# A two-block model on one core: half-row filter products, roots on ScalarE, spread row operations, first head reordered

## The chip, the cores and the metric

The kernel runs on one core of one Trainium2 chip. The metric is device time in microseconds of one execution. The kernel before has a median of 2186.13 us over three runs.

## What is computed

All of it is float32, on 256 rows (latents) and, in the second block, 256 more (context), 1024 columns wide. The first block has two layers of feed-forward, hybrid mixer, feed-forward, each followed by a layer norm; the second has an even layer (a long convolution with a learned filter, and attention) and an odd layer (an mLSTM with eight heads).

```python
for l in range(DEPTH):                                  # first block
    x = layer_norm(ALPHA * x + 0.5 * swiglu(x, w1[l, 0], w2[l, 0]))
    x = layer_norm(ALPHA * x + hybrid_mixer(x, ...))
    x = layer_norm(ALPHA * x + 0.5 * swiglu(x, w1[l, 1], w2[l, 1]))
# second block, layer j:  h = rms_norm(x, g_pre) * (1 + sc) + sh
#   y = even_mixer(h) or odd_mixer(h);  x = x + ga * rms_norm(y, g_post)
def hyena_filter(...):
    hdn = sin(fr * (z @ w1 + b1)); hdn = sin(fr * (hdn @ w2 + b2))
    h = (hdn @ w3).reshape(n, 2, HY_WIDTH)              # w3: 64 x 2048
```

## The kernel before

**Precision.** A large product is made of three matmuls on two parts of each operand: high weights by high features, high by low, low by high. The high part is a rounded copy made on ScalarE (`weights_hi`, line 1497), the low part a subtraction on VectorE (`weights_lo`, line 2071), both for one half block of weights (128 x 2048) at a time. Small products are plain float32, which the trace shows as two passes, each a weight load and a matmul (line 1003).

**Weights and order.** 147 blocks of weights of 2 MB come through a ring of three in the order of use, on SyncE's queue. TensorE's program is one fixed order of half blocks. `after(l, key)` in the programs of ScalarE and VectorE makes the part of the half that takes the slot of the one named; so their place between other work sets when TensorE finds its weights. A half of a block is 48 matmuls of 256 columns or 24 of 512.

**First block.** `ffn` runs eleven pairs of up halves, then eleven down halves (`rows`, line 919). In the mixer VectorE ends the recurrence with `split(hg_hi, hg_lo)`, then runs `rows_gained(l, 0)` (lines 2162 to 2173: the previous norm's gain and bias on two tiles of 1024 columns, four operations in one piece; the end counts `rows_ok`, for which GpSimd waits before it loads the next rows into `bcast`), then the low parts at "yg" 3, 4 and 5. In `ffn` the same piece stands ahead of pair 2. A layer norm takes its root on ScalarE (`row_root`, Sqrt, then a Newton step on VectorE, lines 2116 to 2125).

**Filter network.** `filters(q)` stands between the down halves of the last feed-forward. f1 and f2 are products with 64 output rows, each followed by the sine (range reduction on VectorE, Sin on ScalarE); f3 makes 2 x 4 products of 64 rows into 512 columns (line 1003), for q = 4 and 5.

**Even layer's start.** The roots of the four row tiles come from `root` (lines 2378 to 2389: eleven small VectorE operations, three Newton steps). ScalarE and VectorE scale the rows (`erow`), TensorE transposes them (`turn_all`, line 1097), ScalarE and VectorE make `xt`, ScalarE `x2_hi`, VectorE `x2_lo` (line 2412). `tile_t` (lines 1068 to 1072) then runs high by high and high by low for each k, and the low weights at the end; the first tile waits for `x2_lo` of each k. `x2_hi` lies over the spectra's sources.

**Between the layers.** `post` takes two roots with `root`, the second with the next layer's sums of squares; ScalarE's `squares` and `row_squares` come before. `turn_segment(0)` (line 1111) transposes the rows, `gate_columns` (lines 1349 to 1351) is the first product behind.

**First head.** VectorE computes the gates' logarithm, a low part, waits for `gate_rows` (ScalarE's three copies, in `ml_in(0)`), runs scans (2727 to 2742) with one low part among them, and only then the first head's short convolution (2763 to 2775). ScalarE's Tanh on its result (`ml_silu(0)`) stands at the end of `ml_gates(0)`. Then come the last products for q and k (2779, 2780), `qk_done`, and TensorE's scores (line 1003).

**Start.** Before the first layer VectorE computes softplus of `a_param` as a series of small operations (`log1p`), for which ScalarE runs one Exp.

## Time and profile before

| | before |
|---|---|
| median of three runs | 2186.13 us (2181.99 to 2194.47) |
| profiled execution | 2188.97 us |
| its span | 2187.2 us |
| TensorE matmul, weight load | 2145.6 us (98%), 1945.9 us (89%) |
| VectorE, ScalarE, GpSimd | 1431.6 us (65%), 900.1 us (41%), 18.1 us (1%) |
| moved by DMA | 348.94 MB, mean 160 GB/s |

In the profile PE is TensorE's matmuls, PEld its weight loads, DVE VectorE, ACT ScalarE, POOL GpSimd. Matmuls overlap and their ends are modelled, so a duration in a row is longer than the distance to the next one. A number in square brackets is the idle time ahead of the row and what ended it. PEclk is the share of TensorE's full clock that was granted.

### The profile page before, as it was taken

The numbers are of one execution on the slowest core, as the hardware profiler recorded it, in microseconds if no ns is written. First come the engines' busy times: TensorE is split into PE (matmuls) and PEld (weight loads), VectorE is DVE, ScalarE is ACT, GpSimd is POOL, SyncE is SP. The second block draws the span as 40 slices with busy tenths as digits, with TensorE's granted clock in tenths as the row PEclk, the third lists the DMA queues.
The fourth block names the chain that finished last, engine by engine and source line by source line (L and its number), as shares of the span: only waits on it lengthen the run. The fifth ranks groups of instructions, "written<-read, shape, count | busy, mean of one in ns | idle before, by whom it ended". The sixth has DMA issues, their size and how long they took to land. (4 is left out here: it accounts for less than half of the span.)

```text
span 2187.2 us, 35415 instructions
## 1 busy us (share of the span) xinstructions
PE 2145.6 (98%) x14986; PEld 1945.9 (89%) x14986; DVE 1431.6 (65%) x2084; ACT 900.1 (41%) x1060; POOL 18.1 (1%) x35
## 2 busy tenths in 40 slices
PE   9999999999999999999999999999999989999998
PEld 8998999999989989999899768888788878999996
DVE  5556877685566548876765677877666456666665
ACT  4333365343343334383433353222344334443442
POOL 0000000000000000000000000000000000000000
PEclk9999999999999999999999999999999999999999
DMA  9654555666566555455564432222112232232331
GB/s 346 228 181 186 193 193 200 233 259 232 183 257 235 193 193 191 179 180 203 217 240 185 159 129 77 77 77 77 65 52 78 87 116 78 97 136 78 116 116 58
DMA packets 28925, 348.94 MB, mean 160 GB/s; under 512 B 2976, under 2 KB 5408, under 8 KB 8352
## 3 DMA queue, kind: packets, MB, share of 16 engines
q1 hardware_dynamic: 24672, 313.42, 38.8%
q0 software_dynamic: 4096, 33.26, 3.8%
q8 instruction: 119, 1.95, 0.4%
q14 instruction: 38, 0.31, 0.0%
HBM read 345.62 MB, written 1.05 MB: 158 GB/s over the span
## 5 line engine op out<-in xcount | busy, mean ns | idle before, releaser
L2071 DVE TENSOR_TENSOR w_lo<-ring,w_hi 128x2048 fp32r<-128x2048 f32 x290 | 661.8, 2290 | 417.6 <-ACT w_hi L1497 413.0
L1497 ACT ACTIVATE w_hi<-ring 128x2048 fp32r<-128x2048 f32 x290 | 555.7, 1917 | 700.0 <-PE banks L778 472.3
L773 PE MATMUL banks<-x_hi,w_hi 128*128 128x256 f32 x2112 | 505.2, 280 | 0.2 <-ACT w_hi L1497 0.2
L774 PE MATMUL banks<-x_lo,w_hi 128*128 128x256 f32 x2112 | 504.2, 280 | 0.0
L773 PEld LDWEIGHTS banks<-x_hi,w_hi 128*128 128x128 f32 x2112 | 399.2, 189 | 1.1 <-issue 1.1
L774 PEld LDWEIGHTS banks<-x_lo,w_hi 128*128 128x128 f32 x2112 | 399.5, 189 | 0.0
L778 PE MATMUL banks<-x_hi,w_lo 128*128 128x256 f32 x2112 | 288.8, 279 | 7.9 <-DVE w_lo L2071 7.9
L778 PEld LDWEIGHTS banks<-x_hi,w_lo 128*128 128x128 f32 x2112 | 264.5, 189 | 8.7 <-DVE w_lo L2071 8.7
L1068 PE MATMUL banks<-x_hi,w_hi 128*128 128x512 f32 (+1 forms) x664 | 236.8, 370 | 1.2 <-DVE x_lo L2412 1.2
L1069 PE MATMUL banks<-x_lo,w_hi 128*128 128x512 f32 (+1 forms) x664 | 229.1, 358 | 0.0
L1531 ACT ACTIVATE arena<-banks 128x512 f32<-128x512 f32 (+5 forms) x178 | 79.7, 471 | 284.4 <-PE banks L1072 165.2
L1068 PEld LDWEIGHTS banks<-x_hi,w_hi 128*128 128x128 f32 x664 | 125.1, 188 | 23.2 <-DVE x_lo L2412 3.5
L1072 PE MATMUL banks<-x_hi,w_lo 128*128 128x512 f32 (+1 forms) x664 | 143.6, 358 | 0.8 <-DVE w_lo L2071 0.8
L1069 PEld LDWEIGHTS banks<-x_lo,w_hi 128*128 128x128 f32 x664 | 125.0, 188 | 19.4 <-issue 0.2
L919 PE MATMUL banks<-w_hi,gt_hi 128*128 128x512 f32 x352 | 138.8, 394 | 0.0
L919 PE MATMUL banks<-w_hi,gt_lo 128*128 128x512 f32 x352 | 138.4, 393 | 0.0
L1003 PE MATMUL banks<-arena 128*128 128x256 f32 (+3 forms) x576 | 127.2, 372 | 4.1 <-DVEq L2781 4.1
L1072 PEld LDWEIGHTS banks<-x_hi,w_lo 128*128 128x128 f32 x664 | 111.2, 188 | 21.8 <-DVE w_lo L2071 1.0
L1003 PEld LDWEIGHTS banks<-arena 128*128 128x128 f32 x576 | 99.4, 191 | 25.4 <-issue 9.5
L1082 PE MATMUL banks<-w_hi,x_hi 128*128 128x256 f32 x416 | 103.1, 286 | 0.0
L1083 PE MATMUL banks<-w_hi,x_lo 128*128 128x256 f32 x416 | 100.3, 279 | 0.0
L919 PE MATMUL banks<-w_lo,gt_hi 128*128 128x512 f32 x352 | 89.4, 393 | 0.0
(367 smaller groups left out, 2808.4 us busy)
## 6 DMA issues: line engine op xcount, KB each, us to landing
ring<-weights SPq DMA_DIRECT2D x147, 2048.0 KB, 7.8
arena<-mods POOLq DMA_DIRECT2D x11, 2048.0 KB, 11.6
bcast<-lnrows POOLq DMA_DIRECT2D x12, 512.0 KB, 10.0
ring<-weights SPq DMA_DIRECT2D x2, 1024.0 KB, 9.9
xrow<-x SPq DMA_DIRECT2D x1, 1024.0 KB, 5.2
arena<-hy_consts POOLq DMA_DIRECT2D x1, 1024.0 KB, 15.4
xrow<-ctx_rows POOLq DMA_DIRECT2D x1, 1024.0 KB, 5.3
out<-xrow SPq DMA_DIRECT2D x4, 256.0 KB, 2.0
```

The lines of the kernel that those rows point to most:

```text
L773: nc.tensor.matmul(out, hi[:, k, t * P:(t + 1) * P], x_h[:, k, :], start=k == 0, stop=False)
L774: nc.tensor.matmul(out, hi[:, k, t * P:(t + 1) * P], x_l[:, k, :], start=False, stop=False)
L778: mm = nc.tensor.matmul(out, lo[:, k, t * P:(t + 1) * P], x_h[:, k, :], start=False, stop=k == KT - 1)
L919: mm = nc.tensor.matmul(out, g[:, k, r * P:(r + 1) * P], w[:, u, :], start=k == 0 and p == 0 and not low, stop=k == depth - 1 and low)
L1003: mm = nc.tensor.matmul(out, lhs, rhs, start=n == 0, stop=n == len(pairs) - 1)
L1068: nc.tensor.matmul(out, hi[:, k, part_], x2_hi[:, k, cols_], start=k == 0, stop=False)
L1069: nc.tensor.matmul(out, hi[:, k, part_], x2_lo[:, k, cols_], start=False, stop=False)
L1072: mm = nc.tensor.matmul(out, lo[:, k, part_], x2_hi[:, k, cols_], start=False, stop=k == KT - 1)
L1082: nc.tensor.matmul(out, x2_hi[:, k, rows_], hi[:, k, :], start=k == 0, stop=False)
L1083: nc.tensor.matmul(out, x2_lo[:, k, rows_], hi[:, k, :], start=False, stop=False)
L1497: nc.scalar.activation(hi, raw, ACT.Copy).then_inc(w_hi_done, 1)
L2071: v.tensor_tensor(lo, raw, hi.bitcast(F32), ALU.subtract).then_inc(w_lo_done, 1)
```

## The change

- **Filter network.** The filter weights are loaded twice, into rows 0 to 63 and 64 to 127, by a second DMA on GpSimd's queue; TensorE waits for both. f1 and f2 are computed twice, into either half of the rows of the bank; the sine works on all 128 rows. The f3 products alternate: c = 0 and 2 on the first 64 rows of the array, 1 and 3 on the others.
- **First products.** The first tile of the even layer runs all high by high as `x2_hi` comes, then the low weights, then high by low; `gate_columns` runs both products with `x2_hi` for each k, then high by low.
- **Roots.** `root_of` replaces `root` at three places: ScalarE takes Sqrt (`dev_copy`), VectorE the reciprocal and one Newton step. A Sqrt on one column is put ahead of `squares("even_y", 1)`, an Exp on one column ahead of the gates' exponential.
- **Row operations.** `rows_gained` becomes `row_gained`, one operation behind each of four low parts: pairs 2 and 3 in `ffn`, "yg" 3 and 4 in the mixer.
- **Series.** The softplus series moves from the start to the down halves 0 to 3 of the first feed-forward (`decay_series`), its Exp with it.
- **First head.** `qk_conv(0)` stands ahead of the wait for `gate_rows`, `ml_silu(0)` behind ScalarE's copies in `ml_in(0)`; the head's gate columns stay where they were.

```diff
@@ -733,7 +734,8 @@
-                        pool.dma_start(filt_sb[0:HY_HIDDEN, :], filt).then_inc(S2["hy_in"], 16)
+                        for rows_ in twice:
+                            pool.dma_start(filt_sb[rows_, :], filt).then_inc(S2["hy_in"], 16)
@@ -960,19 +962,22 @@
-                    pe.wait_ge(S2["hy_in"], 48)
+                    pe.wait_ge(S2["hy_in"], 64)
-                    group(banks[0:HY_HIDDEN, b, 0:SEQ], [(hy_w1, hy_zt)], done=b)
+                    group(banks[twice[0], b, 0:SEQ], [(hy_w1, hy_zt)])
+                    group(banks[twice[1], b, 0:SEQ], [(hy_w1, hy_zt)], done=b)
-                    group(banks[0:HY_HIDDEN, b, 0:SEQ], [(hy_w2, sin_out[0])], done=b)
+                    group(banks[twice[0], b, 0:SEQ], [(hy_w2, sin_out[0][twice[0], :])])
+                    group(banks[twice[1], b, 0:SEQ], [(hy_w2, sin_out[0][twice[0], :])], done=b)
-                        group(banks[:, b, :], [(sin_out[1][:, t * P:(t + 1) * P], hy_w3[:, c * 512:(c + 1) * 512])],
+                        group(banks[:, b, :], [(sin_out[1][twice[c % 2], t * P:(t + 1) * P],
+                                                hy_w3[c % 2][:, c * 512:(c + 1) * 512])],
@@ -1062,9 +1067,18 @@
+                if ready is not None:
+                    for k in range(KT):
+                        pe.wait_ge(S2["x2_hi"], k + 1)
+                        nc.tensor.matmul(out, hi[:, k, part_], x2_hi[:, k, cols_], start=k == 0, stop=False)
+                    lo_ready(h)
+                    for k in range(KT):
+                        nc.tensor.matmul(out, lo[:, k, part_], x2_hi[:, k, cols_], start=False, stop=False)
+                    for k in range(KT):
+                        ready(k)
+                        mm = nc.tensor.matmul(out, hi[:, k, part_], x2_lo[:, k, cols_], start=False, stop=k == KT - 1)
+                    return mm
-                    if ready is not None:
-                        ready(k)
@@ -1345,10 +1359,13 @@
+                        pe.wait_ge(S2["x2_hi"], KT + 4 * w + k // 2 + 1)
+                    nc.tensor.matmul(out, gw_hi[:, k, :], x2_hi[:, k, cols_], start=k == 0, stop=False)
+                    nc.tensor.matmul(out, gw_lo[:, k, :], x2_hi[:, k, cols_], start=False, stop=False)
+                for k in range(KT):
+                    if k % 2 == 0:
-                    nc.tensor.matmul(out, gw_hi[:, k, :], x2_hi[:, k, cols_], start=k == 0, stop=False)
-                    nc.tensor.matmul(out, gw_hi[:, k, :], x2_lo[:, k, cols_], start=False, stop=False)
-                    mm = nc.tensor.matmul(out, gw_lo[:, k, :], x2_hi[:, k, cols_], start=False, stop=k == KT - 1)
+                    mm = nc.tensor.matmul(out, gw_hi[:, k, :], x2_lo[:, k, cols_], start=False, stop=k == KT - 1)
@@ -1524,6 +1541,9 @@
+                    if (l, f, q) == (0, 0, 0):
+                        act.wait_ge(sp_abs, 1)
+                        nc.scalar.activation(small[:, 16:32], small[:, 0:16], ACT.Exp).then_inc(sp_exp, 1)
@@ -1660,6 +1678,11 @@
+            def dev_copy(dst, var, n):
+
+                act.wait_ge(S2["root_in"], n)
+                copy(dst, var, S2["root_out"], ACT.Sqrt)
+
@@ -1683,6 +1706,7 @@
+            dev_copy(rs[:, 12:16], rs[:, 24:28], 1)
@@ -1821,6 +1845,8 @@
+                    if (seg, h, r) == ("even_y", 1, 1):
+                        dev_copy(rs[:, 12:14], rs[:, 24:26], 2)
@@ -1830,6 +1856,7 @@
+            copy(floor[:, 0:1], ones[:, 0:1], None, ACT.Sqrt)
@@ -1840,6 +1867,7 @@
+            dev_copy(rs[:, 12:16], rs[:, 24:28], 3)
@@ -1870,6 +1898,7 @@
+            copy(floor[:, 0:1], ones[:, 0:1], None, ACT.Exp)
@@ -1886,6 +1915,7 @@
+                    ml_silu(0)
@@ -1905,7 +1935,6 @@
-                    ml_silu(0)
@@ -2159,24 +2188,23 @@
-            def rows_gained(l, n):
-
-                filled(dve, l, "layer", "turn", n, 3)
-                dve.wait_ge(row_in, 32 * (3 * l + n) + 32)
-                for r in range(RT):
-                    v.tensor_tensor(xrow[:, r, :], xrow[:, r, :], bcast[:, 0, :], ALU.mult)
-                v.drain()
-                for r in range(RT):
-                    x = v.tensor_tensor(xrow[:, r, :], xrow[:, r, :], bcast[:, 1, :], ALU.add)
-                x.then_inc(S2["rows_ok"], 1)
-                v.drain()
+            def row_gained(l, n, r, step):
+
+                if r + step == 0:
+                    filled(dve, l, "layer", "turn", n, 3)
+                    dve.wait_ge(row_in, 32 * (3 * l + n) + 32)
+                v.drain()
+                x = v.tensor_tensor(xrow[:, r, :], xrow[:, r, :], bcast[:, step, :], (ALU.mult, ALU.add)[step])
+                if r + step == 2:
+                    x.then_inc(S2["rows_ok"], 1)
+                    v.drain()
-                    if j == 2 and l + f:
-                        rows_gained(*((l, 1) if f else (l - 1, 2)))
-                    after(l, "up", f, j, 0)
-                    after(l, "up", f, j, 1)
+                    for side in range(2):
+                        after(l, "up", f, j, side)
+                        if j in (2, 3) and l + f:
+                            row_gained(*((l, 1) if f else (l - 1, 2)), side, j - 2)
@@ -2205,25 +2235,44 @@
...
+            def decay_series(step):
+                if step == 0:
+                    v.scalar_tensor_tensor(both(0), ap, -1.0, ap, ALU.mult, ALU.min).then_inc(sp_abs, 1)
+                if step == 1:
+                    dve.wait_ge(sp_exp, 1)
+                if step == 3:
...
@@ -2333,10 +2365,11 @@
-                rows_gained(l, 0)
+                        if q < 5:
+                            row_gained(l, 0, side, q - 3)
@@ -2375,6 +2408,20 @@
+            def root_of(y, v_, d, u, n):
+
+                v.tensor_scalar(u, v_, -0.5, None, ALU.mult)
+                v.drain().then_inc(S2["root_in"], 1)
+                dve.wait_ge(S2["root_out"], n)
+                v.reciprocal(y, d)
+                v.drain()
+                v.tensor_tensor(d, y, y, ALU.mult)
+                v.drain()
+                v.tensor_tensor(d, d, u, ALU.mult)
+                v.drain()
+                v.scalar_tensor_tensor(y, d, 1.5, y, ALU.add, ALU.mult)
+                v.drain()
+
@@ -2395,7 +2442,7 @@
-            root(rs[:, 28:32], rs[:, 24:28], rs[:, 12:16], rs[:, 8:12])
+            root_of(rs[:, 28:32], rs[:, 24:28], rs[:, 12:16], rs[:, 8:12], 1)
@@ -2637,13 +2684,13 @@
-                        root(rs[:, 4:8], rs[:, 24:28], rs[:, 12:16], rs[:, 8:12])
+                        root_of(rs[:, 4:8], rs[:, 24:28], rs[:, 12:16], rs[:, 8:12], 3)
-                        root(y, mean, rs[:, 12:14], rs[:, 14:16])
+                        root_of(y, mean, rs[:, 12:14], rs[:, 14:16], 2)
@@ -2723,6 +2770,25 @@
+            def qk_conv(i):
+                v.tensor_copy(ml_c[:, 0:MLC], c2[:, i * MLC + C2["ml"]:(i + 1) * MLC + C2["ml"]])
+                if i:
+                    head_gates(i)
+                v.drain()
+                released(dve, i, "ml", "q")
...
+                v.drain().then_inc(S2["qk_conv"], 1)
+                dve.sem_inc(S2["copied"], 1)
+            qk_conv(0)
@@ -2760,21 +2826,8 @@
-                v.tensor_copy(ml_c[:, 0:MLC], c2[:, i * MLC + C2["ml"]:(i + 1) * MLC + C2["ml"]])
-                    head_gates(i)
-                v.drain()
...
-                dve.sem_inc(S2["copied"], 1)
+                    qk_conv(i)
```

## Rows read from the trace of the kernel before

**Rows 1.** The page: busy time of each engine, share of the span, instructions.
```profile
PE 2145.6 (98%) x14986; PEld 1945.9 (89%) x14986; DVE 1431.6 (65%) x2084; ACT 900.1 (41%) x1060; POOL 18.1 (1%) x35
```
**Rows 2.** Waits of PE: who waited for whom, us in total, times, longest.
```profile
PE banks L778 <- DVE w_lo L2071: 7.9, 4, 3.6
PE banks L1111 <- ACT arena L1531: 5.4, 1, 5.4
```
**Rows 3.** First head, in order of time: start, us, engine, line, tiles.
```profile
1823.45 1.21 DVE L2727 TENSOR_TENSOR_SCAN arena<-arena 32x512 f32<-32x512 f32 x1 [2.38 <-ACTq L1887]
...
1828.09 2.29 DVE L2071 TENSOR_TENSOR w_lo<-ring,w_hi 128x2048 fp32r<-128x2048 f32 x1
...
1830.44 0.39 PE L1072 MATMUL banks<-x_hi,w_lo 128*128 128x256 f32 x1 [0.83 <-DVE w_lo L2071]
...
1833.95 0.17 DVE L2763 COPY arena<-c 128x10 f32<-128x10 f32 x1 [0.16 <-issue]
...
1839.83 0.48 PE L1003 MATMUL banks<-arena 128*128 128x256 f32 x1 [4.05 <-DVEq L2781]
```
**Rows 4.** Stretches: us, busy (records) of PE, PEld, DVE, ACT, POOL, then PEclk.
```profile
362.20:365.60 3.40, 3.40 (x18) 3.40 (x17) 3.34 (x2) 0.00 (x0) 0.00 (x0) 0.50 0.48 184
365.60:369.00 3.40, 3.40 (x32) 3.40 (x31) 0.24 (x1) 2.19 (x3) 0.00 (x0) 1.00 0.49 96
...
1785.60:1795.80 10.20, 7.43 (x32) 6.85 (x33) 7.57 (x13) 7.41 (x13) 0.00 (x0) 0.50 0.52 223
...
1840.20:1843.60 3.40, 3.40 (x11) 2.74 (x10) 3.32 (x9) 0.00 (x0) 0.00 (x0) 0.50 0.26 111
```
**Rows 5.** Layer 0's mixer, in order of time.
```profile
353.96 2.36 DVE L2167 TENSOR_TENSOR xrow<-xrow,bcast 128x1024 f32<-128x1024 f32 x2
...
358.85 2.29 DVE L2071 TENSOR_TENSOR w_lo<-ring,w_hi 128x2048 fp32r<-128x2048 f32 x1
...
361.19 0.39 PE L778 MATMUL banks<-x_hi,w_lo 128*128 128x256 f32 x1 [3.57 <-DVE w_lo L2071]
```
**Rows 6.** Layer 1's mixer, in order of time.
```profile
991.90 0.39 PE L778 MATMUL banks<-x_hi,w_lo 128*128 128x256 f32 x1 [3.29 <-DVE w_lo L2071]
```
**Rows 7.** Between the layers, in order of time.
```profile
1782.99 0.17 DVE L2380 TENSOR_SCALAR rs<-rs 128x4 f32<-128x4 f32 x1
...
1785.50 1.15 ACT L1531 ACTIVATE arena<-xrow,rs 128x1024 f32<-128x1024 f32 x1 [2.49 <-DVEq L2641]
...
1786.70 3.68 PE L1111 MATMUL banks<-cr,arena 128*128 128x128 f32 x16 [5.43 <-ACT arena L1531]
```
**Rows 8.** A layer norm's root, VectorE in order of time.
```profile
441.00 0.14 DVE L2117 TENSOR_SCALAR rstd<-mv 128x1 f32<-128x1 f32 x1
441.44 0.16 DVE L2121 RECIPROCAL rstd<-rstd 128x1 f32<-128x1 f32 x1 [0.30 <-ACT rstd L1531]
```
**Rows 9.** Even layer's start, ScalarE in order of time.
```profile
1283.53 1.15 ACT L1531 ACTIVATE arena<-xrow,rs 128x1024 f32<-128x1024 f32 x1 [1.61 <-DVEq L2399]
...
1296.58 1.15 ACT L1531 ACTIVATE x_hi<-xt 128x512 fp32r<-128x512 f32 x2
```
**Rows 10.** ScalarE in order of time: a table load, and idle at two places.
```profile
1264.19 1.28 ACT L1531 ACT_TABLE_LOAD   x1
...
1771.20 0.60 ACT L1531 ACTIVATE z<-banks 128x512 f32<-128x512 f32 x1 [0.77 <-PE banks L1262]
...
1813.98 0.26 ACT L1531 ACTIVATE arena<-arena 128x64 f32<-128x64 f32 x1 [3.23 <-DVEq L2704]
```
**Rows 11.** PE in order of time: a filter burst, and the last modulation rows.
```profile
1230.96 3.70 PE L1003 MATMUL banks<-filt_sb,arena 64*128 64x512 f32 x8
...
1779.34 1.93 PE L876 MATMUL banks<-ring,cond 128*2 128x128 f32 x64
```
**Rows 12.** Two stretches of PE alone: us, busy (records), PEclk, DMA share, GB/s.
```profile
250.00:270.00 20.00, 20.00 (x179) 1.00 0.57 211
1170.00:1190.00 20.00, 20.00 (x172) 1.00 0.51 199
```

More of the change, by code:

```diff
@@ L410, in build @@
         top[0] = FT * SEQ * 2
-        sin_out, sin_in = ([part(SEQ)[0:HY_HIDDEN, :] for _ in range(2)] for _ in range(2))
+        sin_out, sin_in = ([part(SEQ) for _ in range(2)] for _ in range(2))
         mod_at = (SBUF_END - arena_at) // 32 * 8 - 512
@@ L447, in build @@
         hy_w2 = filt_sb[0:HY_HIDDEN, SEQ + HY_HIDDEN:SEQ + 2 * HY_HIDDEN]
-        hy_w3 = filt_sb[0:HY_HIDDEN, SEQ + 2 * HY_HIDDEN:FILTCOLS - 4]
+        twice = [slice(HY_HIDDEN * j, HY_HIDDEN * (j + 1)) for j in range(2)]
+        hy_w3 = [filt_sb[rows_, SEQ + 2 * HY_HIDDEN:FILTCOLS - 4] for rows_ in twice]
         hyf = filt_sb[:, FILTCOLS - 4:FILTCOLS]
@@ L1561, in _ @@
             copy(cond[:].rearrange("p a b -> p (a b)"), c2[:, C2["cond"]:C2["cond"] + 16], S2["cond_done"], ACT.Silu)
-            act.wait_ge(sp_abs, 1)
-            nc.scalar.activation(small[:, 16:32], small[:, 0:16], ACT.Exp).then_inc(sp_exp, 1)
             for l in range(DEPTH):
@@ L2195, in ffn @@
                     after(l, "down", f, q // 2, q % 2)
+                    if l + f == 0 and q < 4:
+                        decay_series(q)
                     if q == FT // 4:
@@ L2206, in split, with both @@
                 return v.tensor_tensor(dst_lo, src, dst_hi.bitcast(F32), ALU.subtract)
-            def log1p(dst, y, tmp, tmp2):
-                v.tensor_scalar(tmp, y, 2.0, None, ALU.add)
-                v.drain()
-                v.reciprocal(tmp, tmp)
-                v.drain()
-                v.tensor_tensor(tmp, tmp, y, ALU.mult)
-                v.drain()
-                v.tensor_tensor(tmp2, tmp, tmp, ALU.mult)
-                v.drain()
-                v.tensor_scalar(dst, tmp2, 2.0 / 17.0, 2.0 / 15.0, ALU.mult, ALU.add)
-                for odd in (13.0, 11.0, 9.0, 7.0, 5.0, 3.0, 1.0):
+            lcs = colsb[:].rearrange("p (l c) -> p l c", l=DEPTH)
+            ap = lcs[:, :, LCOL["a_param"]:LCOL["a_param"] + 8]
+            def both(n):
+                return small[:, 16 * n:16 * n + 16].rearrange("p (l k) -> p l k", l=DEPTH)
+            def decay_series(step):
+                dst, y, tmp, tmp2 = (small[:, 16 * n:16 * n + 16] for n in (3, 1, 4, 5))
+                if step == 0:
+                    v.scalar_tensor_tensor(both(0), ap, -1.0, ap, ALU.mult, ALU.min).then_inc(sp_abs, 1)
+                    v.tensor_scalar(half_bs[:], lcs[:, :, LCOL["rg_b"]:LCOL["rg_b"] + 16], 0.5, None, ALU.mult)
+                    v.tensor_scalar(half_ms[:], lcs[:, :, LCOL["b_merge"]:LCOL["b_merge"] + 16], 0.5, None, ALU.mult)
+                    v.tensor_scalar(both(2), ap, -1.0, 0.0, ALU.mult, ALU.max)
+                if step == 1:
+                    dve.wait_ge(sp_exp, 1)
+                    v.tensor_scalar(tmp, y, 2.0, None, ALU.add)
+                    v.drain()
+                    v.reciprocal(tmp, tmp)
+                    v.drain()
+                    v.tensor_tensor(tmp, tmp, y, ALU.mult)
+                    v.drain()
+                    v.tensor_tensor(tmp2, tmp, tmp, ALU.mult)
+                    v.drain()
+                    v.tensor_scalar(dst, tmp2, 2.0 / 17.0, 2.0 / 15.0, ALU.mult, ALU.add)
+                for odd in ((), (), (13.0, 11.0, 9.0, 7.0), (5.0, 3.0, 1.0))[step]:
                     v.drain()
```

48 lines of the change are left out of this document (19 added, 29 removed).

## The prediction

> **What bounds the kernel now.** I read the page first. TensorE is busy 98% of the 2187.2 us span; no other engine passes 65% [rows 1]. So only two things can shorten this kernel: TensorE's own work, and the moments in which it stands still or runs slowly. The chain of waits on the page says the same: it stays on TensorE. Next I listed TensorE's waits by releaser. The reader should see how few and how long they are: four waits of matmuls for the low part of the weights, 7.9 us together, one wait of 5.4 us before the transposes of L1111 [rows 2], one of 4.1 us before the first head's scores [rows 3]. Last I asked for the granted clock around each. After the wait at 361 us, and again after the 5.4 and the 4.1 us waits, it is 0.50, that is 1.2 instead of 2.4 GHz, for 3.4, 10.2 and 3.4 us [rows 4]. A stall is thus paid once in waiting and, mostly, a second time in slow matmuls. Eighteen matmul records stand in the 3.4 us after the first, 32 in the next 3.4: nearly half of such a stretch, 1.7 us, is lost each time that TensorE has dense work to do.
>
> The sum below is made against the profiled execution's own time, 2188.97 us (span 2187.2). The median of the three runs is 2186.13, 2.8 less.
>
> **Row operations, layers' mixers.** Before, `rows_gained(l, 0)` puts four operations on 1024 columns on VectorE in one piece, 353.96 to 358.85, and only then the weights' low part, whose first operation (2.29 us) ends at 361.1; the matmul waits 3.57 us for it and starts at 361.19 [rows 5]. The change puts one row operation (about 1.2 us) behind each of four low parts. The low part then starts at 354.0 and ends at 356.3. TensorE came to it at 361.19 - 3.57 = 357.6, so nothing is left of the wait; the cover left is 1.3 us. The next low part starts 1.2 us after that and ends near 359.8, three microseconds before its use, since one half of a block lasts 5.4 us on TensorE. What is late next there is nothing before the next layer norm. Layer 0 gives 3.6 us and the 1.7 us of clock; layer 1 has the same wait, 3.29 us, without a fall of the clock [rows 6]. In the feed-forward loops the same split hides a block that nobody waited for: none of the long waits is there, so 0. GpSimd's next load of the norm rows waits for `rows_ok`, now some 10 us later; it had to wait only for the next layer norm, over 50 us away, so 0. Sum: **8.6 us**.
>
> **Roots on ScalarE.** The old `root` runs from its first operation at 1782.99 to ScalarE's use at 1785.50: 2.51 us [rows 7]. For the new one the layer norms have the pattern already: from the last scalar operation (441.00) over ScalarE's Sqrt to the reciprocal (441.44) takes 0.44 us [rows 8]. Reciprocal, two products and one more are four steps of 0.25, and the signal to ScalarE 0.28, as in the old one: about 1.5 us. Each root is 1.0 us shorter.
> - First root, before `turn_all`: ScalarE's row copy moves from 1283.53 to about 1282.5 [rows 9]. ScalarE now waits for the deviation ahead of its copies of the second spectrum, so their bank comes free 0.5 us later, about when TensorE wants it. The transposes start 1.0 us earlier.
> - But then the products' new order decides. ScalarE's last high part (the pair begins at 1296.58) ended at 1297.7, and after it the old order had one pair and eight low-weight products left, through 1301.0. The new order has seventeen left, 17 x 0.233 = 4.0 us. With everything 1.0 us earlier this ends at 1300.8: gain **0.2 us**, bounds -0.8 and 1.0.
> - Second and third root, between the layers: the second is off the path, since ScalarE's sums of squares hold up the third. The third starts the transposes 1.0 us earlier (from 1786.70 [rows 7]). The gate columns get the same new order: twelve products instead of six stand behind the last high part. At half clock (0.215 us each) that eats the gain, at full clock about 1.6 us stay. I take **0.5 us**, near the lower end since the stall of over 4 us that remains is still longer than the one at 361 us which lowered the clock; bounds -0.5 and 1.8.
> - New table loads: Sqrt ahead of the second half's squares, Exp ahead of the gates' exponential. A load is 1.28 us; the first meets 0.77 us of idle ahead of the square of 1771.20 and delays that one alone, whose reader is busy with a low part until 1772.7; the second meets 3.23 us of idle [rows 10]. 0.
>
> **First head.** VectorE waited 2.38 us for ScalarE's copies before its scan at 1823.45, and did the head's convolution only at 1833.95, 3.7 us of it (until ScalarE's Tanh at 1837.8); the scores started at 1839.83 after 4.05 us of waiting [rows 3]. The change runs the convolution (3.7 us) in that gap. The scan moves to about 1824.85, 1.4 us later, and with it all behind it on VectorE: the low part of 1828.09, for which TensorE already waited until 1830.44. So the new wait there is about 2.4 us in place of 1.0. Then the head's gates end at 35.3, the two last products of queries and keys at 36.5, while TensorE, 1.4 us later too, wants the scores at 37.05: no wait. Scores start 2.8 us earlier. ScalarE's high parts behind the moved Tanh come 2.3 us later, one of them 0.2 us after TensorE could use it; covered by the same wait. The fall of the clock at 1840.2 [rows 4] goes with its wait, 1.6 us. Sum **4.4 us**; lower bound 2.5, if the wait of 2.4 us pulls the clock down in its turn.
>
> **Filter network.** Eight products of 64 rows run as sixteen passes in two bursts. One burst, from 1230.96, takes 3.70 us by its row, 3.6 without the modelled end of its last pass: eight passes of 0.45 us [rows 11]. The change puts alternate products on the other 64 rows. What two parts of the array do at the same time is seen at L876: 64 passes on four column parts take 1.93 us, where one after the other, at 128 columns each, they would take four times that [rows 11]. If rows behave like columns, 3.6 us become 1.9 (four places of 0.45 and the start of the second part) and both bursts give 3.4 us. Against it stand the two first products, now computed twice: nothing if they overlap, 0.6 us each if not. I take **3.2 us**; bounds -1.2 and 3.4.
>
> The Trainium skill speaks against this term: "TensorE: Matmul & The Clock Gate", Part 3, says that matmuls start and end in strict order. By it the second pass of a product holds back the next product, five slots are needed where four would do, and the term is about 2.4 us. The trace's L876 has two passes to each product and shows no such hold, so I keep the row's value. The page "TensorEngine Tiling (Array Packing)", Key Properties, adds that a change of mode drains the engine; no run here shows that price apart, and the old code changes mode here as often.
>
> **Elsewhere.** The decay series leaves the start for the first down products. No wait of TensorE follows the series at the start, the four of [rows 2] are at 324, 361, 955 and 991 us; and in the down products VectorE has over 3 us free in each 5.5 us half. 0, bounds 0 and 0.3. The second copy of the filter weights is one more load on GpSimd's queue, 90 us ahead of its use. 0.
>
> Sum: 8.6 + 0.2 + 0.5 + 4.4 + 3.2 = 16.9 us. From the profiled time 2172.1; from the median 2169.2. One of the two clock losses that go, in layer 0 but not in layer 1, may be missing in the median run, so I put the forecast between them: **2170.5 us**.
>
> **The rivals.**
> - *The halves of the rows run one after the other, and the head's new wait lowers the clock.* Minus 3.2 and 0.6 more for the doubled products, minus 1.7: 11.4 us gained, 2176.2. For it: no row shows row parts. Chance 0.18.
> - *Matmuls in strict order.* The filter term falls by 0.8 us: 2171.3. By the skill's rule above; against it L876. 0.10.
> - *The pace of the products goes down (slower than before).* The same products run at two paces at full clock: 20 us hold 179 matmul records near 250 us and 172 near 1170 us [rows 12], 4% apart. The pace changes where something short stands between products, so a change of order can move it. Fast stretches of 256 columns are about 410 us of the trace (both mixers mostly); all at the lower pace, with the 512-column ones (365 us, 2%), costs 23 us: 2193. It decides from 17 us on, that is from about three quarters of these stretches. 0.05.
> - *The pace goes up.* About 500 us of feed-forward and mixer go at the lower pace; all at the higher is 19 us less: 2152. 0.05.
> - *The low part is still late in the mixers*, because TensorE runs into a later one: the 8.6 us stay, 2179. Against it the 1.3 us of cover above. 0.06.
>
> **How the numbers follow.** Forecast 0.56, with a range of its own of 2165 to 2176. The rivals at 2176 and 2179 are taken in, the two of the pace for the most part not: **2160 to 2181**. About 0.5%, 11 us, is what a measurement of this kernel tells from no change, so faster means under 2175.2. Faster: forecast and strict order 0.60, a third of the first rival 0.06, pace up 0.05, in all 0.71. Same 0.25. Slower by over 0.5%: 0.04.
>
> **What would show it.** In the changed profile: no matmul of L778 waiting over 1 us near 357 and 984; the granted clock 1.0 there; the passes of a filter burst within 2 us; the first head's long wait replaced by one of 2 to 3 us for the low part, ten microseconds earlier; the wait before the transposes near 4.4 us with the clock still falling; 172 or 179 records in 20 us in the same stretches as before. A lower pace in a mixer, or a new wait for ring loads, would make the prediction wrong.

## The result and the profile after

The changed kernel takes 2170.86 us in the median of 8 runs (2165.54 to 2175.98), the kernel before 2186.22 beside it. The ratio is 0.992, with a 95% interval from 0.9901 to 0.9938: 15.4 us less, where 2170.5 was forecast. The profiled execution took 2168.66 us, its span is 2166.9, so the first pair of profiles lies 20.3 us apart, 5 more than the medians. Where these 5 come from is the first question of the experiments.

TensorE's waits in the changed kernel, by releaser: us in total, times, longest. The two long waits for the low part of [rows 2] are gone, and so is the wait before the first head's scores.

```profile
PE banks L1125 <- ACT arena L1551: 4.3, 1, 4.3
PE banks L792 <- ACT w_hi L1514: 2.3, 1, 2.3
PE banks L1086 <- DVE w_lo L2100: 2.1, 1, 2.1
PE banks L1073 <- ACT x_hi L1551: 2.0, 2, 1.1
...
PE banks L1363 <- ACT x_hi L1551: 1.8, 2, 1.2
...
PE banks L780 <- DVE w_lo L2100: 1.0, 2, 0.5
```

L1125 is the old L1111, 5.4 before; the 2.1 us are the first head's new wait. The two rows of 2.0 and 1.8 us are new: they wait for ScalarE's high parts, in the two places where the order of the products was changed.

VectorE in layer 0's mixer. The row operations of [rows 5] now stand one behind each low part, and each low part ends before its use.

```profile
353.10 2.29 DVE L2100 TENSOR_TENSOR w_lo<-ring,w_hi 128x2048 fp32r<-128x2048 f32 x1
355.48 1.22 DVE L2197 TENSOR_TENSOR xrow<-xrow,bcast 128x1024 f32<-128x1024 f32 x1
356.62 2.28 DVE L2100 TENSOR_TENSOR w_lo<-ring,w_hi 128x2048 fp32r<-128x2048 f32 x1
359.00 1.23 DVE L2197 TENSOR_TENSOR xrow<-xrow,bcast 128x1024 f32<-128x1024 f32 x1
```

Stretches of the changed kernel: us, busy (records) of PE, PEld, DVE, ACT, POOL, then PEclk, DMA share, GB/s. Where TensorE stood still before, in layer 0's mixer, the clock is 1.00. But in the even layer's first tile there is a fall that the kernel before did not have, and between the layers the clock is down for 13.7 us and not 10.2 [rows 4].

```profile
354.00:358.00 4.00, 4.00 (x37) 4.00 (x37) 3.91 (x3) 2.65 (x3) 0.00 (x0) 1.00 0.63 266
...
1279.60:1283.00 3.40, 3.40 (x10) 2.63 (x9) 2.40 (x4) 2.09 (x3) 0.00 (x0) 0.51 0.02 5
1767.70:1781.40 13.70, 10.52 (x47) 9.90 (x48) 10.05 (x30) 9.48 (x14) 0.00 (x0) 0.50 0.50 213
```

A filter burst in the changed kernel, and the doubled first product. Eight passes take 1.92 us to the next matmul, where [rows 11] had 3.6; four passes of f1 have 0.65 us, against 0.64 for the two before.

```profile
1193.18 0.65 PE L1008 MATMUL banks<-filt_sb 33*64 33x256 f32 x4
```
```profile
1216.73 1.99 PE L1008 MATMUL banks<-filt_sb,arena 64*128 64x512 f32 x8
1218.65 0.50 PE L921 MATMUL banks<-w_hi,gt_hi 128*128 128x512 f32 x1
```

**Where the time went.** I set each matmul of one trace beside the same matmul of the other and took the difference of their starts. From it I took out the pace of the products: what a product of 256 columns takes over 113.3 ns, or one of 512 over 229, when it lies within 110 to 122 or 225 to 240 ns. That pace alone is 32.2 us in the first profile of the kernel before and 27.5 in the changed one's. The rest, in us ahead of the first profile of before (the three columns ahead of the last are experiments below; the line "all" also holds 0.4 us less between 950 and 985 us in all four, which is the first profile's own):

```
stretch                        forecast  b_again  b_rows  b_filt_head  changed
start, to 345 us                  0.0      0.5     -0.1       0.1        0.6
layer 0's mixer                   5.3     -0.9      5.5       0.0        5.5
layer 1's mixer                   3.3     -2.9      3.6      -1.6        3.6
filter network                    3.2      0.0      0.0       3.4        3.4
even start: to the transposes     1.0      0.0      0.0       0.0        1.2
even start: first tile           -0.8      0.0      0.0       0.0       -2.4
between layers: to transposes     1.0      0.0      0.0       0.0        1.2
between layers: gate columns     -0.5      0.4      0.1      -0.2       -1.5
first head, from 1803 us          4.4     -0.8      0.0       4.3        4.4
all, with what lies between      16.9     -4.5      8.6       6.0       15.6
pace of the products              0.0      4.3      4.7       6.3        4.7
```

So the 20.3 us of the first pair are 15.6 us of changes and 4.7 of pace.

Two things on how to read the runs below. They were taken in five sets on several chips, each with runs of the kernel before beside it; the ratio is always to those. And the medians of the same changed kernel in two sets differ by 5.7 us, so a term of one to three microseconds is read from the traces, not from a median.

### The profile page after: what moved, and what is told of

Same layout as the page of the kernel before. It is cut to its first block, busy times and chain, and to the rows that moved or that the text cites. A ratio compares the mean times of both kernels' runs of the same rounds, so it can differ in the third digit from the quotient of the medians.

```text
span 2166.9 us, 35416 instructions
## 1 busy us (share of the span) xinstructions
PE 2136.0 (99%) x14990; PEld 1938.4 (89%) x14990; DVE 1429.6 (66%) x2066; ACT 902.2 (42%) x1066; POOL 18.8 (1%) x36
## 4 chain that ended last, share of the span: by engine, by line
PE 94%; DVE 2%; ACT 2%; DVEq 1%; issue 0%; ACTq 0%
PE banks L921 13%; PE banks L780 12%; PE banks L775 12%; PE banks L776 12%; PE banks L1008 8%; PE banks L1086 6%; PE banks L1083 6%; PE banks L1082 6%; PE banks L792 2%; PE banks L1100 2%; PE banks L1096 2%; PE banks L1097 2%; PE banks L1277 2%; PE banks L1276 2%; PE banks L1278 2%; PE banks L878 1%
```

## The experiments

**The kernel before, once more.** No edit.

> The kernel before, unchanged, profiled once more. In the first pair of profiles the changed kernel is 20.3 us ahead, in the medians 15.4. 4.5 us of the 20.3 come in the feed-forward loops, where no order changed and only the distance of the products differs (114.8 against 117.8 ns). Theory A, the pace is a draw of each execution: this profile shows other stretches at the lower pace than the first one, its span differs from 2187.2 by up to 5 us, and aligned with the first profile the difference lies in the feed-forward loops. Theory B, the pace belongs to the program: the same stretches, and the span within 1 us of 2187.2. In both, the fall of the clock after the 3.5 us wait of the first layer's mixer: there again by theory of a rule (a wait of that length always lowers it), gone by the theory that it depends on the phase.

Measured: 2188.43 us (12 runs, 2184.51 to 2191.91), ratio 1.0011 (0.9999 to 1.0022). The same stretch of the same program, first in the first profile, then in this one (columns as above):

```profile
660.00:680.00 20.00, 20.00 (x172) 20.00 (x172) 16.12 (x12) 6.78 (x6) 1.05 (x2) 1.00 0.50 176
```
```profile
660.00:680.00 20.00, 20.00 (x179) 20.00 (x178) 15.24 (x14) 8.48 (x6) 1.05 (x2) 1.00 0.48 172
```

The reader should see 172 and 179 matmul records at the same granted clock: the pace of a stretch can differ between two executions of one program, as theory A says. It happens that the spans agree to 0.1 us, since 4.3 us of better pace stand against 4.5 of other losses. Of these, 3.8 us went in the mixers to falls of the clock: after the wait in layer 0's mixer it was down for 6.8 us instead of 3.4, and after the one in layer 1's for 6.8 where the first profile had none. And there was a wait that the first profile lacks, of 1.8 us at the start:

```profile
33.81 0.85 PE L778 MATMUL banks<-x_hi,w_lo 128*128 128x256 f32 x5 [1.80 <-DVE w_lo L2071]
```

VectorE was at the decay series until 31.4 us. In this execution the clock rose earlier in the first microseconds (0.8 us gained) and did not fall at 14 us (1.6 us): TensorE was 2.4 us further by 18 us, and so it ran into the series.

**The changed kernel, once more.** No edit.

> The changed kernel, unchanged, profiled once more. Theory A (pace is a draw): span 2162 to 2173, other stretches at the lower pace than in its first profile. Theory B (pace belongs to the program): span within 1 us of 2166.9, same stretches. The fall of the clock in the first tile of the even layer (1279.6, 3.4 us at 0.50) and the 13.7 us at 0.50 between the layers: both again if the new orders of products cause them, one of them missing if they hang on the phase.

Measured: 2165.12 us (4 runs, 2163.95 to 2166.81), ratio 0.9911 (0.9894 to 0.9928). The span is 2165.0. The pace differs in the first 200 us; from there on nearly the same stretches are at the lower pace as in the first profile, and the sums are 27.4 and 27.5 us. That half of theory A's forecast failed: the pace can differ between executions, but here it mostly repeated. The 1.9 us between the spans are the start. Both falls are there again, 3.4 us in the first tile and 13.7 between the layers. The clock stayed up at the start, TensorE was 2.0 us ahead at 20 us, and kept it: there is no wait at 33 us here. All 12 runs of the changed kernel together have a median of 2167.7 us; its distance from before is 15.4 us in one set and 20.6 in the other.

**The row operations alone.** Before, with:

```diff
-                rows_gained(l, 0)
                 for q in (3, 4, 5):
                     for side in range(2):
                         after(l, "yg", q, side)
+                        if q < 5:
+                            row_gained(l, 0, side, q - 3)
```
(and the same in the feed-forward).

> The kernel before with the row operations spread, and nothing else. My theory: the waits of 3.6 and 3.3 us for the low part in the two mixers are gone, nothing is late in their place; aligned with a profile of the kernel before, 3.6 us (5.3 where that profile has a fall of the clock there) are gained in layer 0's mixer, 3.3 in layer 1's, 0 in the feed-forward loops beside the pace of the products. In time 7 to 9 us less than before. Rival: the spread is what moved the pace in the feed-forward loops of the changed kernel (4.5 us): then the loops are faster here too, in all 11 to 14 us less.

Measured: 2175.38 us against 2185.74, ratio 0.9956 (0.9941 to 0.9971), 10.4 us less. By the trace 5.5 and 3.6 us, and 0 in the feed-forward loops once the pace is taken out. The rival falls: the pace here (27.5 us) is also that of the untouched kernel's second profile (27.9). That the median gained more than 8.6 would fit the falls after layer 1's wait (of the three traces with the old mixer, the next experiment's being the third, two have one there), but six runs do not show it.

**Filter network and first head alone.** Before, with the diff's edits of `filters`, of the filter weights' DMAs and of the sine, and with these lines, whose old places are emptied:

```diff
+            qk_conv(0)
             dve.wait_ge(S2["gate_rows"], 1)
...
                     A.drain().then_inc(S2["gate_rows"], 1)
                     act.sem_inc(free[b], 1)
+                    ml_silu(0)
```

> The kernel before with the filter network's halves and the first head's new order, and nothing else; the two lie 600 us apart and are read apart in the trace. My theory: the filter bursts take 1.9 us each instead of 3.6 and the doubled first products cost nothing, 3.4 to 3.5 us gained; the first head gains 3.9 to 4.5 us (scores without a wait, the low part's wait 2.1 instead of 0.8), and no fall of the clock. In time 7 to 8 us less than before. Rival for the head: without the roots' change in front the head starts in another phase, the 2.1 us wait lowers the clock, and only 2.5 us remain.

Measured: 2178.31 us against 2185.74, ratio 0.9972 (0.9957 to 0.9987), 7.4 us less. By the trace the filters give 3.4 us and the head 4.3; the wait of 2.1 us did not lower the clock. Both as expected. The two filter bursts:

```profile
1226.24 1.99 PE L1008 MATMUL banks<-filt_sb,arena 64*128 64x512 f32 x8
...
1233.87 1.99 PE L1008 MATMUL banks<-filt_sb,arena 64*128 64x512 f32 x8
```

**The old orders of products.** The changed kernel, with:

```diff
-                if ready is not None:
-                    for k in range(KT):
-                        pe.wait_ge(S2["x2_hi"], k + 1)
...
                 for k in range(KT):
+                    if ready is not None:
+                        ready(k)
                     nc.tensor.matmul(out, hi[:, k, part_], x2_hi[:, k, cols_], start=k == 0, stop=False)
                     nc.tensor.matmul(out, hi[:, k, part_], x2_lo[:, k, cols_], start=False, stop=False)
```
(and `gate_columns` as before).

> The changed kernel with the old order of products in both places: the first tile of the even layer takes high by high and high by low together and the low weights last, and so do the gate columns. The roots on ScalarE stay. Theory A, the new orders cost the two losses (first tile -2.4 us behind transposes that start 1.15 earlier, gate columns -1.5 behind transposes 1.15 earlier): aligned with the changed kernel, 2.0 to 2.4 us are gained in the first tile, half of it since the clock does not fall there, and 0.5 to 1.2 between the layers, where the stretch at 0.50 is back to 10.2 us. Theory B, the clock falls there by the phase alone: it falls here too and at most 0.6 us are gained in the first tile.

Measured: 2166.77 us (6 runs, 2157.45 to 2172.48), ratio 0.9916 (0.9894 to 0.9938). Against the changed kernel's trace 2.4 us are gained in the first tile and 1.6 between the layers, where the clock is down for 10.2 us again: theory A. The median shows none of it: it lies between those of the changed kernel's two sets (2165.12 and 2170.86). In the trace, 1.6 us went at another place, where the clock fell after the first head's 2.1 us wait; how often it does so in the unprofiled runs is not known.

```profile
1804.70:1808.10 3.40, 3.40 (x19) 3.40 (x18) 2.96 (x6) 0.42 (x1) 0.00 (x0) 0.53 0.00 0
```

**The three kinds of product interleaved.** The changed kernel, with:

```diff
-                    for k in range(KT):
-                        pe.wait_ge(S2["x2_hi"], k + 1)
...
+                    for k in range(0, KT, 2):
+                        for a in (k, k + 1):
+                            pe.wait_ge(S2["x2_hi"], a + 1)
+                            nc.tensor.matmul(out, hi[:, a, part_], x2_hi[:, a, cols_], start=a == 0, stop=False)
...
+                        for a in (k, k + 1):
+                            nc.tensor.matmul(out, lo[:, a, part_], x2_hi[:, a, cols_], start=False, stop=False)
+                        for a in (k, k + 1):
+                            ready(a)
+                            mm = nc.tensor.matmul(out, hi[:, a, part_], x2_lo[:, a, cols_], start=False, stop=a == KT - 1)
```
in the first tile; `gate_columns` takes each pair's high by low once the next pair's products with the high part are issued.

> The changed kernel with the three kinds of product interleaved by pairs of k in both places, so that after ScalarE's last high part only six products are left in the first tile (16 in the changed kernel) and eight in the gate columns (12). If TensorE has work at hand between the high parts, its waits of 0.9 and 1.1 us in the first tile mostly fill and the clock stays at 1.00: the first tile ends 3.5 to 4.5 us earlier than in the changed kernel, the gate columns 0.8 to 1.5 us. If the clock falls all the same: 2.5 and 0.8. Time 3 to 5 us below the changed kernel.

Measured: 2166.13 us (6 runs, 2161.3 to 2179.52), ratio 0.992 (0.9893 to 0.9947). First tile 4.4 us earlier, no fall there. Gate columns 0.1, not 0.8 to 1.5: the clock is down for 13.7 us, as in the changed kernel. Half the expectation failed, and the median is not 3 to 5 us below the 2167.7 of the changed kernel's 12 runs. The clock fell after the head's wait here too.

**Order of the last filter products, and the series back at the start.** The changed kernel, with:

```diff
-                        group(banks[:, b, :], [(sin_out[1][twice[c % 2], t * P:(t + 1) * P],
-                                                hy_w3[c % 2][:, c * 512:(c + 1) * 512])],
+                        part = 0 if t else c // 2
+                        group(banks[:, b, :], [(sin_out[1][twice[part], t * P:(t + 1) * P],
+                                                hy_w3[part][:, c * 512:(c + 1) * 512])],
```
and `decay_series(0..3)` before the first layer.

> The changed kernel with two edits 1200 us apart. First, the order of the last filter products: in the first burst the two products of the first half of the rows stand next to each other, then the two of the second half; in the second burst all four are on the first half. Halves that work at the same time only when neighbours in the program differ (strict order): first burst 3.0 to 3.6 us, with one overlap in the middle; halves that run ahead of each other freely: 1.9 us as in the changed kernel. Second burst 3.6 us in either case, 1.7 more. Second edit, the decay series is back before the first layer: no wait of TensorE changes there, 0; the 0.6 us which the changed kernel was ahead at 20 us stay or go with the clock's phase and not with the series.

Measured: 2172.56 us against 2184.67, ratio 0.9944 (0.9924 to 0.9964). The two bursts:

```profile
1220.19 1.99 PE L1009 MATMUL banks<-filt_sb,arena 64*128 64x512 f32 x8
1222.11 0.51 PE L921 MATMUL banks<-w_hi,gt_hi 128*128 128x512 f32 x1
...
1227.83 3.70 PE L1009 MATMUL banks<-filt_sb,arena 64*128 64x512 f32 x8
1231.46 0.50 PE L921 MATMUL banks<-w_hi,gt_hi 128*128 128x512 f32 x1
```

With the products of one half next to each other in the program the burst takes the same 1.92 us: the halves run ahead of each other. All on one half takes 3.63. The second edit went against the expectation of 0. As in the untouched kernel's second profile the clock stayed up at the start, TensorE reached the low part early, and waited for the series; then the clock fell: TensorE was 2.4 us ahead of the first profile of before at 30 us and 2.2 behind at 40, so 4.6 us were lost.

```profile
34.19 1.08 PE L780 MATMUL banks<-x_hi,w_lo 128*128 128x256 f32 x7 [2.79 <-DVE w_lo L2100]
```

**The roots back on VectorE.** The changed kernel, with `root` for `root_of` at the three places, and without `dev_copy` and the two operations on one column.

> The changed kernel with all three roots back on VectorE and without the two table loads ahead; the new orders of products stay. Each root is 1.0 us longer, the transposes start 1.15 us later in both places. First tile: its end is set by ScalarE's last high part and the 16 products behind it, so 1.0 to 1.2 us are lost, and the fall of the clock stays if the order of the products is its cause. Between the layers 1.0 to 1.2 us are lost in the wait before the transposes (5.4 instead of 4.3), and no gain stands against it. Rival: ScalarE's wait for the deviation was itself a cost, and less than 0.6 is lost at the first place.

Measured: 2171.76 us against 2184.67, ratio 0.9938 (0.9918 to 0.9958). The transposes start 1.0 us later at the first place and 1.15 at the second: the rival falls. But the first tile then ends 0.6 us ahead of the changed kernel's, since with the same new order the clock did not fall:

```profile
1278.60:1283.00 4.40, 3.51 (x11) 1.70 (x9) 3.99 (x8) 3.82 (x8) 0.00 (x0) 1.00 0.00 0
```

Between the layers the low clock came in two pieces, 3.4 and 6.8 us, and the gate columns lost 2.0 us behind the transposes, where the changed kernel lost 1.5.

So the fall in the first tile costs 1.6 us and the order by itself 0.8. The order makes it likely, not certain: four traces have the new order there and three of them the fall; of five with the old order and five interleaved none has it.

**Toward a better kernel.** The changed kernel with the interleaved first tile (first edit of a_inter) and the old gate columns (second edit of a_order).

> The changed kernel with the first tile's products interleaved by pairs of k and the gate columns in their old order. What two runs gained apart should add: 4.4 us in the first tile (no fall of the clock there) and 1.6 between the layers (10.2 us at 0.50 instead of 13.7), 6 us against the changed kernel beside the pace of the products and the falls of the clock elsewhere. In time 2160 to 2165 us. If the gate columns' gain hung on the phase of the clock and not on the order, only 4.4.

Measured: 2166.26 us (5 runs, 2164.46 to 2168.55), ratio 0.9915 (0.9902 to 0.9928). Against the changed kernel's trace 4.4 us are gained in the first tile and 1.0 between the layers, not 1.6 (10.2 us at the low clock); the pace was 2.4 us worse and the start 0.5.

**The wait between the layers filled.** The same, with (the products write a bank that the transposes then overwrite):

```diff
             mod_row(8, 0)
-            turn_segment(0)
+            take(pe, 0, "odd", "pre", 0, 0)
+            for _ in range(36):
+                nc.tensor.matmul(banks[:, plan["odd"]["pre", 0, 0][0], 0:P], ident, ident, start=True, stop=True)
+            turn_segment(0, True)
```
(`True`: the bank is already taken).

> As the kernel with both of these orders, and 36 products of 128 columns whose result nobody reads fill TensorE's wait of 4.3 us between the layers. If the wait is what lowers the clock, it stays at 1.00 through the transposes and the gate columns: the transposes take 1.9 us instead of 3.7, the twenty-four products of each half run at 0.12 instead of 0.215 us, and behind ScalarE's and VectorE's steps 2.5 to 4 us are left at the first products of the next layer. If the clock falls all the same, the fillers change nothing, or cost up to 1 us where they outlast the wait.

Measured: 2170.96 us, ratio 0.9933 (0.9918 to 0.9948). The clock stays at 1.00, but each filler is two passes: they last 8.2 us and delay the transposes by 3.8. From there to the first products of the next layer 3.0 us are gained on the changed kernel, against 1.0 without fillers; in all it is 1.8 us behind the kernel without fillers, and the median too is higher.

**The same fillers, the gate columns interleaved.**

> The kernel with both places interleaved, and the same 36 products in the wait between the layers. At the full clock the order of the gate columns costs nothing any more: the old order waits 1.7 us for the low part first, the interleaved one starts with ScalarE's high part and has eight products left behind the last. If the clock stays at 1.00 it is 0 to 1 us ahead of the filled kernel with the old order; if the new order lowers the clock by itself (its waits lie between products), it falls during the gate columns and 1 to 2 us are lost.

Measured: 2164.95 us, ratio 0.9915 (0.9897 to 0.9933). From the transposes 2.2 us are gained, 0.8 less than with the old order: the clock falls for 3.4 us at 1770, in the gate columns. That is the second outcome, but one trace does not show that the order does it: with the old order TensorE waits longer there, in two pieces of 2.2 and 1.4 us, and the clock stayed up. The waits in the gate columns, first here, then in the next experiment's trace:

```profile
PE banks L1368 <- ACT x_hi L1556: 3.1, 2, 1.9
```
```profile
PE banks L1368 <- DVE x_lo L2722: 3.6, 2, 2.5
```

The median goes the other way than the 0.8 us, 6 us below that of the fillers with the old order. In the two traces the pace makes 6.1 us in that direction; that the same holds in the other runs is not shown.

**Half as many fillers, old gate columns.**

```diff
-            for _ in range(36):
+            for _ in range(18):
```

> The filled kernel with 18 instead of 36 products. The 36 ran as 72 passes of 0.113 us, 8.2 us, and delayed the transposes by 3.8; eighteen take 4.1 us and end inside the wait of 4.3. If the clock stays at 1.00 as it did with 36: transposes on time, then 1.7 us gained in them, and 1.0 to 1.5 in the gate columns, in all 2.7 to 3.2 us against the changed kernel between 1762 and 1787 us, where the kernel with the same orders and no fillers gained 1.0. If a shorter filling lets the clock fall all the same: 1.0 as without fillers. The first tile gains its 4.4 us again. In time 2160 to 2165 us, since the pace of the products moves single executions by more than these terms.

Measured: 2160.5 us (4 runs, 2153.66 to 2161.56) against 2187.05, ratio 0.9876 (0.9858 to 0.9895). That is 26.5 us below the kernel before. The changed kernel was not run beside it; its ratios were 0.992 and 0.9911, so this one is probably faster, by four runs. The fillers and the transposes, TensorE in order of time, and the stretch behind:

```profile
1751.11 4.29 PE L1356 MATMUL banks<-cr 128*128 128x128 f32 x36
1755.47 1.97 PE L1127 MATMUL banks<-cr,arena 128*128 128x128 f32 x16
```
```profile
1756.50:1770.00 13.50, 9.93 (x83) 9.54 (x82) 10.69 (x31) 9.49 (x14) 0.00 (x0) 1.00 0.33 139
```

The transposes start on time and take 1.97 us instead of 3.68 [rows 7]; 2.9 us are gained there and 4.4 in the first tile. Without fillers the same orders gained 1.0, so filling the wait is worth 1.9 us. This trace, of the fastest of the four runs, is 15.0 us ahead of the changed kernel's first: beside these, 7.0 us are pace and 2.1 a start without a fall, and 1.6 are lost by a fall after the first head's wait.

## Why the forecast came out

The median was met to 0.4 us, the sum only in part, and that closeness is luck in three ways. The forecast took about 1.3 us off the sum because layer 0's fall of the clock might be missing in the median run; the runs gave no reason for that (in b_again the clock was down after both mixers' waits, for 6.8 us each, and b_rows gained 10.4 us in the median). The two reordered places gave 2.2 us less than forecast, and nobody expected the small gains elsewhere. And the sample: the changed kernel's second set has 2165.12. Point by point:

- **Row operations.** Right in mechanism and size: 5.5 and 3.6 us for 5.3 and 3.3, b_rows alone, nothing late behind. What the argument from one profile missed is that the fall after such a wait is not a property of the place: layer 1's wait of 3.3 us had none in the first profile, 3.4 us in b_filt_head's and 6.8 in b_again's. The median's 10.4 would fit that.
- **Filter network.** The row value of L876 was the right one to take: 3.4 us for 3.2, in all ten traces with alternating halves. The rival of rows that run one after the other falls, and so does strict order. The Trainium skill's rule that matmuls start and end in program order ("TensorE: Matmul & The Clock Gate", Part 3) does not hold for a_f3_series: in program order the second half's first product could not start before the first half's second one, and the burst would need six places of 0.45 us, or seven if the order holds pass by pass: an estimate of 2.7 to 3.2 us, where 1.92 were measured. The doubled first products cost 0.01 us. (The first rival's sum took 0.6 us for them once; by the term's own bounds it is 0.6 us for each of two, which would have made it 0.6 us slower.)
- **First head.** Right step by step. VectorE's scan was forecast 1.4 us later and came 1.4 later; the new wait was given 2.4 us and measured 2.07; the scores start without one.

VectorE (DVE) and TensorE in the changed kernel's first head, to be read against [rows 3]:

```profile
1808.77 1.22 DVE L2793 TENSOR_TENSOR_SCAN arena<-arena 32x512 f32<-32x512 f32 x1 [0.21 <-issue]
...
1813.40 2.29 DVE L2100 TENSOR_TENSOR w_lo<-ring,w_hi 128x2048 fp32r<-128x2048 f32 x1
```
```profile
1815.75 1.21 PE L1086 MATMUL banks<-x_hi,w_lo 128*128 128x256 f32 x8 [2.07 <-DVE w_lo L2100]
...
1821.15 1.99 PE L1008 MATMUL banks<-arena 128*128 128x256 f32 x8
```

  What the lower bound was for, that the clock falls after this wait in its turn, happened in 4 of the 11 traces that have the wait, for 1.6 us each time.
- **First root and first tile.** Forecast 0.2, measured -1.2, below the bound of -0.8. The roots' part was right (1.0 forecast, 1.2 measured), and so was the count of products behind the last high part. The step that failed is that these 17 products were priced at 0.233 us, at the full clock. Between the high parts TensorE has less to do in the new order: its two waits there grew from 0.37 and 0.80 us (for VectorE's low part) to 0.89 and 1.12 (for ScalarE's high part), the clock fell, and the low-weight products took 0.40 us each. With the clock up, in a_root, the same order cost 0.8 us, as forecast:

```profile
1278.45 1.02 PE L1073 MATMUL banks<-x_hi,w_hi 128*128 128x512 f32 x2 [1.12 <-ACT x_hi L1551]
1279.31 3.42 PE L1076 MATMUL banks<-x_hi,w_lo 128*128 128x512 f32 x8
1282.53 2.21 PE L1079 MATMUL banks<-x_lo,w_hi 128*128 128x512 f32 x8
```

- **Between the layers.** Forecast 0.5, measured -0.3, within its bounds. The transposes start 1.15 us earlier. But I took the clock's return as given: with the new or the interleaved order it came back for good 11.9 to 13.3 us after the transposes' start in five traces, with the old order after 3.7 to 11.0 in six. What in the order does that stays open: TensorE's waits inside the gate columns sum to 1.8 us in the changed kernel and to 1.7 in a_order.
- **Decay series.** Forecast 0, with a bound of 0.3, and wrong for a share of the executions. "No wait follows the series" was read from a profile whose clock fell at 14 us. Where it does not fall, TensorE comes 2.0 to 2.4 us earlier, and the wait for the series takes 2.0 us of the lead (b_again), or 4.6 with the fall of the clock behind it (a_f3_series); with the series moved, the five traces without the fall at 14 us keep their lead. That fall follows a wait of 2.3 us for ScalarE at 13 us, which all 14 traces have; it came in seven. In these seven the clock had first risen at 6.3 to 7.5 us, in the other seven at 4.3 to 5.7.
- **Pace.** The two rivals of the pace were framed wrongly: as an effect of the edit, with a sign. It can differ from one execution of a program to the next (32.2 and 27.9 us for the kernel before) and can repeat (27.5 and 27.4 for the changed one). Over 14 traces it is 20.3 to 32.6 us over the quicker of the two, and it put 4.7 us into the first pair of profiles. The chip alone does not decide it: four traces from one chip have 20.3 to 32.6 us, four from another 20.5 to 31.4. What does is open; it changes mostly where something short stands between products, but not each time.

Sum against trace: 15.6 us for 16.9. The two reordered places gave 2.2 us less; against it stand 0.9 us of small differences elsewhere (0.6 at the start, 0.5 in the mixers, 0.2 in the filter network, less the 0.4 of the first profile).

## What to carry to other kernels

A wait that one profile does not show is not absent: ask what the bound engine meets when it comes two microseconds earlier. When products are reordered around a late operand, look at the waits between the operands: in the first tile they grew, the clock fell in three of four traces, and interleaving (five traces, no fall) gained 4.4 us. It is no general cure: in the gate columns the interleaved order gained 0.1 us. Where a wait of several microseconds before dense work can't be removed, products that nobody reads kept the clock up in all three traces that had them; count their passes first, so that they end inside the wait (36 products outlasted a wait of 4.3 us by 3.8, 18 did not).

## What the runs showed of the hardware

- Two halves of the array's rows worked at the same time, for float32 products of 64 rows (1.92 us for 3.63). Of their order in the program, alternating and two by two were measured, and both took 1.92 us.
- At a granted clock of 1.00 the same products of the same program ran at 113 or at 118 ns (256 columns) in long stretches, and the stretches can differ from one execution to the next.
- The length of a wait alone did not decide whether the clock fell after it: it did after 2.1 us in 4 of 11 traces, after 2.3 us in 7 of 14, after 3.3 us in two of three, after 3.6, 3.9 to 4.1 and 4.3 to 5.4 us in all traces that have those waits unfilled (three, three and eleven traces). After two waits of 0.9 and 1.1 us within 3 us it fell in three of four; with two of 2.2 to 2.5 and 1.1 to 1.4 us behind fillers it stayed up in both traces.
- A fall of 3.4 us cost 1.6 us at each of four places where a trace with it and one without could be compared (start, layer 1's mixer, first tile, first head).
